# A PEER layer with a ring of five gathered rows and three load slots, in place of six and two

## What is computed

```python
def peer_ffn(x, w_q, sub_keys, u, v):        # u, v: 16384 experts x 1024
    ...
    def block_fn(xb):
        q = (xb @ w_q).reshape(blk, PEER_HEADS, 2, PEER_HALF)
        s = jnp.einsum('thcd,hcnd->thcn', q, sub_keys).astype(jnp.float32)
        s_top, i_top = lax.top_k(s, PEER_TOPK)
        cand_s = (s_top[:, :, 0, :, None] + s_top[:, :, 1, None, :]).reshape(blk, PEER_HEADS, -1)
        cand_e = (i_top[:, :, 0, :, None] * N_KEYS + i_top[:, :, 1, None, :]).reshape(blk, PEER_HEADS, -1)
        best_s, best_pos = lax.top_k(cand_s, PEER_TOPK)
        expert = jnp.take_along_axis(cand_e, best_pos, axis=-1)
        gate = jax.nn.softmax(best_s, axis=-1)
        act = jax.nn.gelu(jnp.einsum('td,thkd->thk', xb, u[expert]).astype(jnp.float32), approximate=False)
        return jnp.einsum('thk,thkd->td', (gate * act).astype(xb.dtype), v[expert])
```

## Time and profile before

| | |
|---|---|
| median of 3 runs | 5255.7 us |
| the profiled execution | 5254.98 us |
| its span, first to last instruction | 5253.1 us |
| PE busy | 4308.1 us (82%) |
| DVE busy | 3096.9 us (59%) |
| POOL busy | 1920.2 us (37%) |
| gathers' DMA queue (software) | 679.04 MB, 34.4% of 16 engines' span |
| loads' DMA queue (hardware) | 416.69 MB, 22.6% |

### The profile page before, as it was taken

The page is one execution under the profiler, slowest core; times in us unless marked ns, Lnnn a source line. Parts: engine busy times, 40 slices in busy tenths (PEclk is TensorE's granted clock), DMA queues, the critical chain, the costliest instruction groups (busy, mean ns, idle before and its releaser), DMA issues. The chain is left out here.

```text
span 5253.1 us, 56097 instructions
## 1 busy us (share of the span) xinstructions
PE 4308.1 (82%) x21158; PEld 3533.7 (67%) x21158; DVE 3096.9 (59%) x5685; ACT 1026.1 (20%) x2272; POOL 1920.2 (37%) x1559
## 2 busy tenths in 40 slices
PE   6989679788997559996787799996888997469995
PEld 5467438577886458885555688863677886458884
DVE  1315540599957796656216633345599867796656
ACT  0102310222332150000012222211222332150000
POOL 0000230166657624444002433312256557614444
PEclk9985669899998779998878788858899998779997
DMA  2330112488889948998111000013588889939998
GB/s 91 89 75 1 34 37 96 167 301 313 311 338 397 369 128 342 409 396 348 56 58 35 1 1 1 1 41 104 188 300 310 319 341 390 363 109 371 409 399 333
DMA packets 403487, 1099.26 MB, mean 209 GB/s; under 512 B 70508, under 2 KB 157261, under 8 KB 402886
## 3 DMA queue, kind: packets, MB, share of 16 engines
q0 software_dynamic: 186496, 679.04, 34.4%
q1 hardware_dynamic: 216726, 416.69, 22.6%
HBM read 1066.88 MB, written 32.45 MB: 209 GB/s over the span
## 5 line engine op out<-in xcount | busy, mean ns | idle before, releaser
L1036 DVE SCALAR_TENSOR_TENSOR gg_ytok<-gg_ring,gg_gw,gg_ytok 128x1024 f32<-128x1024 f32 x320 | 422.1, 1319 | 178.5 <-DMA gg_ring<-in_peer_v,gg_idx 172.5
L1036 DVE SCALAR_TENSOR_TENSOR fg_ytok<-fg_ring,fg_gw,fg_ytok 128x1024 f32<-128x1024 f32 x320 | 422.0, 1319 | 176.6 <-DMA fg_ring<-in_peer_v,fg_idx 170.0
L706 POOL DMA_INDIRECT fg_ring<-in_peer_u,fg_idx x320 | 377.2, 1179 | 351.7 <-DVE fg_ring L1030 284.4
L706 POOL DMA_INDIRECT gg_ring<-in_peer_u,gg_idx x320 | 374.4, 1170 | 345.7 <-DVE gg_ring L1030 275.9
L1030 DVE SCALAR_TENSOR_TENSOR fg_ring<-fg_ring,fg_htok 128x1024 f32<-128x1024 f32 x320 | 409.7, 1285 | 128.1 <-DMA fg_ring<-in_peer_u,fg_idx 126.4
L1030 DVE SCALAR_TENSOR_TENSOR gg_ring<-gg_ring,gg_htok 128x1024 f32<-128x1024 f32 x320 | 409.8, 1286 | 127.8 <-DMA gg_ring<-in_peer_u,gg_idx 125.7
L774 PE MATMUL fg_bank<-f_hTd,fg_uT 128*128 128x256 f32 x2048 | 476.9, 387 | 0.6 <-ACT f_buf L873 0.6
L774 PE MATMUL gg_bank<-g_hTd,gg_uT 128*128 128x256 f32 x2048 | 476.2, 387 | 0.6 <-ACT g_buf L873 0.6
L706 POOL DMA_INDIRECT gg_ring<-in_peer_v,gg_idx x320 | 358.1, 1119 | 272.1 <-DVE gg_ytok L1036 211.8
L706 POOL DMA_INDIRECT fg_ring<-in_peer_v,fg_idx x320 | 345.7, 1080 | 276.3 <-DVE fg_ytok L1036 214.4
L774 PEld LDWEIGHTS fg_bank<-f_hTd,fg_uT 128*128 128x128 f32 x2048 | 389.8, 196 | 51.2 <-issue 0.9
(11 more groups left out here) (620 smaller groups left out, 7758.8 us busy)
## 6 DMA issues: line engine op xcount, KB each, us to landing
fg_ub<-in_peer_u SPq DMA_DIRECT2D x128, 512.0 KB, 6.8
gg_ub<-in_peer_u SPq DMA_DIRECT2D x128, 512.0 KB, 6.7
fg_ub<-in_peer_v SPq DMA_DIRECT2D x64, 512.0 KB, 7.2
fg_uT<-in_peer_v SPq DMA_DIRECT2D x64, 512.0 KB, 6.7
gg_ub<-in_peer_v SPq DMA_DIRECT2D x64, 512.0 KB, 7.3
gg_uT<-in_peer_v SPq DMA_DIRECT2D x64, 512.0 KB, 6.8
f_buf<-in_peer_w_q SPq DMA_DIRECT2D x16, 1024.0 KB, 12.2
g_buf<-in_peer_w_q SPq DMA_DIRECT2D x16, 1024.0 KB, 11.8
```

The source lines that it names most:

```text
L706: pool.indirect_dma_start(ring[:, n % RING, :], None, (u_rows if kind == "u" else v_rows)[:, :], bass.IndirectOffsetOnAxis(ap=idx[:, r:r + ...
L1036: dve.scalar_tensor_tensor(ytok[:, :], row, gw[:, r:r + 1], ytok[:, :], ALU.mult, ALU.add).then_inc(used, 1)
```

## The change

The ring of gathered rows has five slots instead of six, and `ub` three instead of two, so that the sum is eight slots of 512 KB as before. The slots of v are those of `ub` and the halves of `uT`, hence five instead of four. All waits and all numbers that depend on the slots follow: a gather waits for unit n - 5, a load of u for the transposes of block b - 3, a load of v for the product of block b - 5.

```diff
+NRING = 5
+NUB = 3
+NVB = NUB + 2
...
-        ring = ph.sb("ring", [P, RING, D])
-        ub = ph.sb("ub", [P, 2, D])
+        ring = ph.sb("ring", [P, NRING, D])
+        ub = ph.sb("ub", [P, NUB, D])
...
-        vb = [ub[:, 0, :], ub[:, 1, :], uTf[:, 0:D], uTf[:, D:2 * D]]
+        vb = [ub[:, k, :] for k in range(NUB)] + [uTf[:, 0:D], uTf[:, D:2 * D]]
...
-                load_u(0)
-                load_u(1)
+                for b in range(NUB):
+                    load_u(b)
...
-                    if key[0] == "b" and key[1] + 3 <= nblk:
+                    if key[0] == "b" and key[1] + NUB < nblk:
                         b = key[1]
                         sp.wait_ge(t_half, 2 * b + 2)
-                        load_u(b + 2)
-                for b in range(4):
+                        load_u(b + NUB)
+                for b in range(NVB):
                     if b == 0:
                         sp.wait_ge(t_half, 2 * nblk)
-                    if b == 2:
+                    if b == NUB:
                         sp.wait_ge(gm_done, NGC)
...
-                    sp.wait_ge(o_done, b - 3)
+                    sp.wait_ge(o_done, b - NVB + 1)
...
-                    while looks and n >= units_before_hit[looks[0]] + RING:
+                    while looks and n >= units_before_hit[looks[0]] + NRING:
...
-                    if n >= RING:
-                        pool.wait_ge(used, n - RING + 1)
+                    if n >= NRING:
+                        pool.wait_ge(used, n - NRING + 1)
```

More of the change, by code:

```diff
@@ L515, in peer_layer @@
         w_in = [ph.sem("w_in0"), ph.sem("w_in1")]
-        u_in = [ph.sem("u_in0"), ph.sem("u_in1")]
-        v_in = [ph.sem(f"v_in{k}") for k in range(4)]
+        u_in = [ph.sem(f"u_in{k}") for k in range(NUB)]
+        v_in = [ph.sem(f"v_in{k}") for k in range(NVB)]
         k_in, x_in, y_out = ph.sem("k_in"), ph.sem("x_in"), ph.sem("y_out")
@@ L529, in peer_layer @@
         a_zero, fold_mm, fold_ev = ph.sem("a_zero"), ph.sem("fold_mm"), ph.sem("fold_ev")
-        landed = [ph.queue_sem(f"landed{k}") for k in range(RING)]
+        landed = [ph.queue_sem(f"landed{k}") for k in range(NRING)]
         h_in, a_in, a_out = ph.queue_sem("h_in"), ph.queue_sem("a_in"), ph.queue_sem("a_out")
@@ L630, in load_u @@
                 def load_u(b):
-                    sp.dma_start(ub[:, b % 2, :], uv[:, b, :]).then_inc(u_in[b % 2], 16)
+                    sp.dma_start(ub[:, b % NUB, :], uv[:, b, :]).then_inc(u_in[b % NUB], 16)
                 sp.dma_start(kin[:, :, :], sub_keys.rearrange("h c n d -> n (h c) d")).then_inc(k_in, 16)
@@ L643, in _ @@
                             load_w(n + 2)
-                    if key[0] == "b" and key[1] + 3 <= nblk:
+                    if key[0] == "b" and key[1] + NUB < nblk:
                         b = key[1]
                         sp.wait_ge(t_half, 2 * b + 2)
-                        load_u(b + 2)
-                for b in range(4):
+                        load_u(b + NUB)
+                for b in range(NVB):
                     if b == 0:
                         sp.wait_ge(t_half, 2 * nblk)
-                    if b == 2:
+                    if b == NUB:
                         sp.wait_ge(gm_done, NGC)
                     sp.dma_start(vb[b], vv[:, b, :]).then_inc(v_in[b], 16)
-                for b in range(4, nblk):
-                    sp.wait_ge(o_done, b - 3)
-                    sp.dma_start(vb[b % 4], vv[:, b, :]).then_inc(v_in[b % 4], 16)
+                for b in range(NVB, nblk):
+                    sp.wait_ge(o_done, b - NVB + 1)
+                    sp.dma_start(vb[b % NVB], vv[:, b, :]).then_inc(v_in[b % NVB], 16)
                 sp.wait_ge(o_done, nblk)
@@ L703, in _ @@
                         pool.wait_ge(kt_quad, 4)
-                    if n >= RING:
-                        pool.wait_ge(used, n - RING + 1)
-                    pool.indirect_dma_start(ring[:, n % RING, :], None, (u_rows if kind == "u" else v_rows)[:, :],
+                    if n >= NRING:
+                        pool.wait_ge(used, n - NRING + 1)
+                    pool.indirect_dma_start(ring[:, n % NRING, :], None, (u_rows if kind == "u" else v_rows)[:, :],
                                             bass.IndirectOffsetOnAxis(ap=idx[:, r:r + 1], axis=0)
-                                            ).then_inc(landed[n % RING], 16)
+                                            ).then_inc(landed[n % NRING], 16)
                     for k in range(2):
-                        if n == last_u[k] + RING - 1:
+                        if n == last_u[k] + NRING - 1:
                             pool.wait_ge(used, last_u[k] + 1)
                             load_h(k + 1)
-                        if n == last_v[k] + RING - 1:
+                        if n == last_v[k] + NRING - 1:
                             pool.wait_ge(used, last_v[k] + 1)
@@ L759, in turn @@
                 def turn(b):
-                    pe.wait_ge(u_in[b % 2], 16 * (b // 2 + 1))
+                    pe.wait_ge(u_in[b % NUB], 16 * (b // NUB + 1))
                     for c in range(2):
@@ L765, in turn @@
                             d = 4 * c + k
-                            last = pe.transpose(pt[:, c, k, :], ub[:, b % 2, d * P:(d + 1) * P], ident[:, :])
+                            last = pe.transpose(pt[:, c, k, :], ub[:, b % NUB, d * P:(d + 1) * P], ident[:, :])
                         last.then_inc(t_half, 1)
@@ L804, in _ @@
                 for b in range(nblk):
-                    pe.wait_ge(v_in[b % 4], 16 * (b // 4 + 1))
+                    pe.wait_ge(v_in[b % NVB], 16 * (b // NVB + 1))
                     for d in range(KD):
-                        last = pe.matmul(out[:, d // 2, (d % 2) * TD:(d % 2 + 1) * TD], vb[b % 4][:, d * P:(d + 1) * P],
+                        last = pe.matmul(out[:, d // 2, (d % 2) * TD:(d % 2 + 1) * TD], vb[b % NVB][:, d * P:(d + 1) * P],
                                          hidden[:, b, :], start=(b == 0 and d % 2 == 0), stop=(b == nblk - 1 and d % 2 == 1),
@@ L1009, in gathered @@
                     kind, r = order[n]
-                    row = ring[:, n % RING, :]
+                    row = ring[:, n % NRING, :]
                     k = min(r // SLOTS, 2)
@@ L1027, in gathered @@
                         dve.wait_ge(used, at["v", r - 1] + 1)
-                    dve.wait_ge(landed[n % RING], 16 * (n // RING + 1))
+                    dve.wait_ge(landed[n % NRING], 16 * (n // NRING + 1))
                     if kind == "u":
```

## The result

The changed kernel takes 5366.88 us (median of 6 runs, 5362.17 to 5385.68), the kernel before, beside it on the same chip, 5265.22 us (6 runs, 5235.42 to 5281.68). The ratio is 1.0177, with a 95% interval of 1.0154 to 1.0199: slower, and outside the range of 5225 to 5325 us.

A forecast was written before the change was run, and what follows sets the result against it. The stream of 640 gathers through POOL, DMA and DVE was taken as the bound. Ring costs of 29.6 us per layer, 59.2 in two, less 41.75 for the hole gave +17.5 us: 5272 us, range 5225 to 5325 us.

The forecast's parts named there:

- The hole: DVE's 19.0 and 22.75 us standstills at the selection's last Exp close with a third u slot: -41.75 us together.
- PE's waits for u: In the selection, each of PE's five waits for a load of u shrinks by 4.33 us with the third slot.
- Ring of five, selection: In the top-k selection, one gather of 1.85 us is lost in each of seven passes: 13.0 us per layer.
- the selection loses in every chunk: Rival: a gather lost at all three places of a selection pass, 38.9 us per layer; +69 us, 5324 us; chance 0.13.
- Gathers alone on the DMA: Where no loads run beside the gathers, each of 104 gathers takes 0.10 us more: 10.4 us per layer.
- Gathers beside loads of u: From 4240 to 4541 us, each of 124 gathers takes 0.05 us more, 1.84 us each: 6.2 us per layer.
- V stage: In the v stage the DMA engines stay full at 2.08 us per gather, so five ring slots cost 0.
- The first rival: Landing times are no queue, so the ring paces all stretches: 123 us per layer, +204 us, 5459 us; chance 0.06.
- the third: Rival: five loads of u move into idle DMA time in the selection, ring costs nothing: -55.4 us, 5200 us; chance 0.05.
- The estimate that the prediction worked out from the rule of the Trainium skill: 3.2 us per 512 KB gather, so ring costs for gathers alone and beside loads of u are 0; sum 5239 us.

## Why the prediction was wrong

*The hole* was right: Exp in time, DVE without a wait, -22.7 and -19.0 us. But I put the whole gain down to the third slot. The ring alone closes it as well, so the two edits' effects don't add.

*PE's waits for u* were to shrink by 4.33 us each, from between 6.62 and 10.28 us; three are left, 1.43, 3.87 and 1.40 us long. They shrank by more than that, from 43.4 to 6.7 us in all, since the smaller ring made PE late as well: the third slot alone left 17.4 us, the smaller ring alone 32.2 us. So this step held, but it did not bring the stream forward: the 172nd unit was to end 13 us later and the 200th 6 to 10 us earlier; they ended 34.4 and 28.9, 12.7 and 11.3 us later.

*Ring of five, selection* is the step that failed most. I took 13.0 us per layer, one lost gather a pass, and it measured 34.4 and 28.9 us: 37.4 us more over both layers. The ring alone makes 27.5 and 23.7 us of this. The other 6.9 and 5.2 us come with the third slot, whose earlier loads of u I had counted at nothing (with a ring of six they cost 14.1 and 8.8 us).

The rival "the selection loses in every chunk" came nearer, with 38.9 us. I argued against it that the twenty gathers of the earlier trace rows pass two steps and still come every 1.85 us; that is a rate, and a rate does not show whether DVE waits. My count was wrong too: I had three places in a pass, while DVE's list has up to five chunks in each, 33 in a layer. The place to look was the length of a chunk beside the depth of the ring: 19 chunks have six or seven units, a ring of five can hold five, and the waits stand just past the depth, at the sixth unit with five slots and at the fifth with four. The run with short chunks took the waits at the sixth unit away. But that is only a part of the ring's price here: some 14 us of waits in a layer stay with chunks of five, and where these come from stays open.

*Gathers alone on the DMA* failed too. I had POOL's wait for the slot fall from 1.2 to 0.3 us, hence 0.10 us per gather. It stayed at a median of 1.1 us, the mean falling only from about 1.1 to 0.85 us, and landing stayed at 6.0 us; a gather takes 1.72 us instead of 1.50. In the kernel before POOL set the pace of 1.40 us there: 1.09 us per issue and a gap of 0.30 us. The two groups of POOL's issues in that stretch, before:

```profile
L706 POOL DMA_INDIRECT gg_ring<-in_peer_u,gg_idx x15 | 16.8, 1121 | 4.6 <-issue 4.6
L706 POOL DMA_INDIRECT gg_ring<-in_peer_v,gg_idx x15 | 15.8, 1053 | 6.3 <-issue 4.3 <-DVE gg_ytok L1036 2.1
```

and after:

```profile
L709 POOL DMA_INDIRECT gg_ring<-in_peer_v,gg_idx x13 | 14.9, 1144 | 7.9 <-DVE gg_ring L1033 5.2 <-issue 2.7
L709 POOL DMA_INDIRECT gg_ring<-in_peer_u,gg_idx x12 | 14.8, 1235 | 7.2 <-DVE gg_ytok L1039 5.4 <-issue 1.8
```

Behind the bar stand busy time and mean duration, then the idle time and what ended it. Before, nearly all of it is the gap between two issues; after, 10.6 us are waits for DVE to release a slot. POOL no longer sets the pace, but its issues are longer still (1144 and 1235 ns), because DVE's units hold them (below), so that it is often late for a released slot all the same.

Together with the next term the rest of the u stage grew by 23.7 and 23.9 us instead of 13.6, and the last 40 units by 5.2 and 4.5 us instead of 3.0.

*Gathers beside loads of u* had the right round by luck: between the 200th and 300th unit a gather took 1.86 to 1.87 us, against my 1.84, but the parts were others. Landing was 7.1 us on average there (8.2 before), not 7.7, and POOL took a released slot after 0.87 us, not 0.3. And before, a gather took 1.75 to 1.76 us there, not 1.79, so the loss is 0.11 us, twice my term.

*V stage*: right in its main point, full DMA share and landing at 8.7 us; the 6.1 and 3.7 us that it lost were not counted, and what they are I did not settle. The argument was weaker than it looked: with a ring of four the share is full too, and the stage loses 33.1 and 33.8 us. The first rival, 71 us a layer in this stage, falls with it, and the third is excluded, since the rest of the u stage grew.

The sum: 70.7 us more than the +17.5 us forecast, of which the selection has 37.4, the rest of u 20.4, the v stage 9.8 and the last 40 units 3.6 us, less 0.5 us in the one-hot stage. The estimate that the prediction worked out from the rule of the Trainium skill ("DMA: Bandwidth & Descriptors", section "Anatomy of one DMA — SWDGE (gpsimd) path"), that five slots would be ample, does not hold here: each slot taken away cost time, a ring of four 6.5%.

## What to carry to other kernels

Compare the depth of a ring with the longest burst that its consumer takes, not with the mean rate alone: the unit just past the depth waited 1.2 us on average here (23.4 us at 19 sixth units), 0.5 us with one slot more. But try the remedy on the old depth as well: shorter bursts took 19 us of waits away with five slots and 12 to 14 us with six, so most of that gain had nothing to do with the smaller ring. Write a ring's round out part by part, and count the issuing engine's delays in it, since these need not shrink with the depth. And before adding up the gains of two edits, ask whether one of them alone already makes the other's wait disappear.

## What was unexpected of the hardware

POOL's issue of a gather takes 0.94 us while DVE is idle, but longer while DVE runs a unit. The timeline of the changed kernel with gathers alone:

```profile
4653.55 1.22 DVE L1033 SCALAR_TENSOR_TENSOR gg_ring<-gg_ring,gg_htok 128x1024 f32<-128x1024 f32 x1
4653.72 1.86 POOL L709 DMA_INDIRECT gg_ring<-in_peer_u,gg_idx  x1 [0.72 <-DVE gg_ytok L1039]
...
4655.82 1.32 DVE L1039 SCALAR_TENSOR_TENSOR gg_ytok<-gg_ring,gg_gw,gg_ytok 128x1024 f32<-128x1024 f32 x1 [1.04 <-DMA gg_ring<-in_peer_v,gg_idx]
4655.88 0.94 POOL L709 DMA_INDIRECT gg_ring<-in_peer_v,gg_idx  x1 [0.30 <-issue]
```

The first issue begins 0.17 us into DVE's unit and ends 0.81 us after the end of that unit, as if it had begun only then. Six more between 4657 and 4670 us begin 0.15 to 1.0 us into a unit, and all end 0.80 to 0.82 us after its end. The last issue shown begins 0.06 us after a unit and is not held. Over 30 gathers with a ring of four, issues that start within a unit take 1.40 to 1.47 us on average and the others 0.94 us. With DVE's units cut to 64 columns nearly all take 0.94 us, which shows that it is the unit that holds them. It is so throughout: in both layers of the two kernels and of the ring of four, 964 of the 966 issues that begin 0.11 to 1.05 us into a unit take over 1.0 us and end 0.80 to 0.85 us after it, and of the 1770 that begin on an idle DVE none takes more than 0.99 us.

The Trainium skill, "SBUF — State Buffer", section "Who interferes with whom", has a rule for this: a DVE instruction with two inputs in SBUF contends with a GpSimd instruction that reads SBUF, for ports that act as an exclusive lock, so that whichever is second is held until the other is done. The trace agrees for an indirect DMA, which reads its indices (`gg_idx`) from SBUF, in the seven cases of held issues. Two instructions of the one-hot stage, each with two inputs, agree as well, counted over the same three runs: the comparison with both inputs in SBUF (L1066 of the changed kernel) holds all 12 issues that begin in it, 1.68 to 1.97 us, and the multiplication that takes one input from PSUM, the memory that PE writes to (`gg_bank`, L1057), none of 135, 0.94 us at most. The last issue shown, which a unit just begun does not hold, is not explained by the rule.

A gather lands in 4.2 us in the one-hot stage, where the DMA engines are busy 40% of the time. With the gathers alone on the DMA and the ring turning, it takes 5.4 to 6.0 us, whether the ring has four, five or six slots. What sets that figure stays open.
